# Gate weight blocks of a SwiGLU stage multiplied as seven half-size products instead of eight

## The reference

```python
def swiglu(x, w_gate, w_up, w_down):            # x: 512 x 1024, w_gate and w_up: 1024 x 2816, w_down: 2816 x 1024
    return (jax.nn.silu(x @ w_gate) * (x @ w_up)) @ w_down

x = x + 0.5 * swiglu(rms_norm_2(x, ffn1_norm[layer]), ...)
```

## Time and profile before

| | |
|---|---|
| median of 3 runs | 2524.61 us (2520.6 to 2525.54) |
| profiled execution, its own time | 2523.24 us |
| its span in the trace | 2521.4 us |
| granted TensorE clock | 0.996 of full speed |
| TensorE matmul busy | 2482.9 us, 98% |
| VectorE busy | 1000.6 us, 40% |
| ScalarE busy | 865.6 us, 34% |
| GpSimd busy | 1069.8 us, 42% |

### The profile page before, as it was taken

The page is one execution under the profiler, slowest core; times in us unless marked ns, Lnnn a source line. Parts: engine busy times, 40 slices in busy tenths (PEclk is TensorE's granted clock), DMA queues, the critical chain, the costliest instruction groups (busy, mean ns, idle before and its releaser), DMA issues.

```text
span 2521.4 us, 31320 instructions
## 1 busy us (share of the span) xinstructions
PE 2482.9 (98%) x12983; PEld 2048.2 (81%) x12983; DVE 1000.6 (40%) x1664; ACT 865.6 (34%) x1286; POOL 1069.8 (42%) x830
## 2 busy tenths in 40 slices
PE   8999999999999999999999999999999999999999
PEld 7889778876688888887788888888888888888887
DVE  5676445145572222456532222421313544322222
ACT  4433443246552222336632222422212322322221
POOL 4233345312254444433244444544444544444443
PEclk9999999999999999999999999999999999999999
DMA  4122103210143233312132332233332333233322
GB/s 143 60 68 94 34 26 118 84 51 20 49 129 100 88 98 99 94 57 72 44 105 96 99 101 92 92 101 101 100 100 72 112 100 100 84 100 101 100 89 79
DMA packets 215863, 217.66 MB, mean 86 GB/s; under 512 B 10615, under 2 KB 213106, under 8 KB 215722
## 3 DMA queue, kind: packets, MB, share of 16 engines
q1 hardware_dynamic: 215520, 215.61, 27.0%
q10 hardware_dynamic: 202, 0.06, 0.0%
HBM read 213.53 MB, written 2.12 MB: 86 GB/s over the span
## 4 chain that ended last, share of the span: by engine, by line
PE 94%; DVE 3%; ACT 2%; issue 1%; DMA 0%; SPq 0%; DVEq 0%; ACTq 0%
PE ps L516 73%; PE ps L509 6%; PE ps L519 5%; PE ps L513 2%; PE ps L869 2%; PE ps L904 1%; PE ps L886 1%; PE ps L2137 1%; PE ps L2198 1%; PE ps L1638 1%; ACT wh L475 0%; PE ps L538 0%; PE ps L1983 0%; PE ps L2003 0%; DVE NL L626 0%
## 5 line engine op out<-in xcount | busy, mean ns | idle before, releaser
L490 POOL TENSOR_TENSOR wl<-raw,wh 128x512 fp32r<-128x512 f32 x794 | 1040.0, 1342 | 1397.3 <-ACT wh L475 1382.9
L516 PE MATMUL ps<-NH,wh 128*128 128x512 f32 (+1 forms) x1824 | 716.3, 393 | 1.6 <-DVE NL L626 1.5
L516 PE MATMUL ps<-NL,wh 128*128 128x512 f32 (+1 forms) x1824 | 712.2, 390 | 0.0
L516 PE MATMUL ps<-NH,wl 128*128 128x512 f32 (+1 forms) x1824 | 711.9, 390 | 0.0
L475 ACT ACTIVATE wh<-raw 128x2048 fp32r<-128x2048 f32 (+3 forms) x218 | 378.9, 1738 | 475.1 <-PE ps L516 422.6
L516 PEld LDWEIGHTS ps<-NH,wh 128*128 128x128 f32 (+1 forms) x1824 | 343.0, 188 | 79.5 <-issue 6.4
L516 PEld LDWEIGHTS ps<-NL,wh 128*128 128x128 f32 (+1 forms) x1824 | 342.8, 188 | 73.7 <-issue 1.4
L516 PEld LDWEIGHTS ps<-NH,wl 128*128 128x128 f32 (+1 forms) x1824 | 342.7, 188 | 72.6
L516 PE MATMUL ps<-GH,wh 128*128 128x512 f32 x824 | 323.1, 392 | 0.0
L516 PE MATMUL ps<-GH,wl 128*128 128x512 f32 x824 | 320.7, 389 | 0.0
L516 PE MATMUL ps<-GL,wh 128*128 128x512 f32 x824 | 320.7, 389 | 0.0
(11 more groups left out here) (419 smaller groups left out, 2907.8 us busy)
## 6 DMA issues: line engine op xcount, KB each, us to landing
raw<-in_ffn_w_gate SPq DMA_DIRECT2D x44, 1024.0 KB, 5.3
raw<-in_ffn_w_up SPq DMA_DIRECT2D x44, 1024.0 KB, 5.3
raw<-in_ffn_w_down SPq DMA_DIRECT2D x32, 1024.0 KB, 5.1
raw<-in_w_in_ab SPq DMA_DIRECT2D x15, 1024.0 KB, 5.4
raw<-in_w_in_cd SPq DMA_DIRECT2D x14, 1024.0 KB, 5.0
raw<-in_ffn_w_down SPq DMA_DIRECT2D x16, 768.0 KB, 4.3
raw<-in_c_w_in SPq DMA_DIRECT2D x12, 1024.0 KB, 5.1
raw<-in_w_out_ab SPq DMA_DIRECT2D x8, 512.0 KB, 3.5
```

The source lines that it names most:

```text
L490: nc.gpsimd.tensor_tensor(wl[:, b % 2, ks, 0:w], raw[:, b % 2, ks, 0:w], wh[:, b % 2, ks, 0:w].bitcast(F32), ALU.subtract).then_inc(S("wei ...
L516: last = nc.tensor.matmul(ps[0:m1 - m0, bank, 0:SEQ], w[:, s, k, m0:m1], x(k), start=start, stop=stop)
```

## The change

From the third pair of a stage on (`SEVEN_FROM = 4` column tiles), the nine gate blocks of each of the four stages get the form "S". Such a block (1024 rows x 256 columns) is cut in four quarters A11 to A22 of 512 rows x 128 columns, the tokens' operand in four quarters B11 to B22 of 512 rows x 256 tokens. The two-by-two block product is formed from seven quarter products, with the sums S1 to S4 of the A quarters and T1 to T4 of the B quarters, instead of eight.

- The sums of weights are made for every S block: two by POOL, two by DVE. ACT then takes seven high parts, POOL seven low parts, of 128x512 elements each.
- The sums of tokens are made once a stage: eight tiles `bf` (H times the gain) by ACT, four differences by DVE, four high parts by ACT, four low parts by DVE, all in the time of the first two pairs, which keep the old form.
- TensorE adds the products into banks 0, 1 and 2. ACT copies the bank between products (`seven_copy`, three copies of 128x256 into `xs`), and DVE adds these later (`seven_dve`).
- ACT's list of a pair with an S block following: high parts of the next gate block now stand before the silus, and `seven_copy` of the next gate block stands behind the `GH` copies and ahead of the high part of the next up block.
- The F gates move to banks 0 and 1, the up units to 6 and 7, the down units of the first two groups to 4 to 7. The final gain of stage 0 moves from pairs 0 to 3 to pairs 2 and 3, four tiles in each.

The diff, without the buffers' places, the operand slices and the plain renamings of counts:

```diff
+LEFT = ("A11", "S1", "S2", "S4", "S3", "A12", "A22")
+RIGHT = ("B11", "T1", "T2", "B22", "T3", "B21", "T4")
+ACCUMULATOR = (0, 1, 0, 1, 0, 2, 0)
...
+            taken = (bank, bank + 1) if b.form == "W" else (0, 1, 2) if b.form == "S" else (bank,)
...
+    def seven_sums_pool(pool, b):
+        pool.wait_ge(S(f"raw_ready_{b % 2}"), RAWC[b])
+        nc.gpsimd.tensor_tensor(ssum[:, 2, :, :], seven_raw(b, "A11"), seven_raw(b, "A21"), ALU.subtract).then_inc(S("gate_sum"), 1)
+        nc.gpsimd.tensor_tensor(ssum[:, 0, :, :], seven_raw(b, "A21"), seven_raw(b, "A22"), ALU.add).then_inc(S("gate_sum"), 1)
+
+    def seven_sums_dve(dve, b):
+        n = SEVENS.index(b)
+        dve.wait_ge(S("gate_sum"), 2 * n + 1)
+        nc.vector.tensor_tensor(ssum[:, 1, :, :], seven_raw(b, "A22"), ssum[:, 2, :, :], ALU.subtract).then_inc(S("gate_mix"), 1)
+        dve.wait_ge(S("gate_mix"), 2 * n + 1)
+        nc.vector.tensor_tensor(ssum[:, 3, :, :], seven_raw(b, "A12"), ssum[:, 1, :, :], ALU.subtract).then_inc(S("gate_mix"), 1)
+
+    def seven_high(act, b):
+        n = SEVENS.index(b)
+        act.wait_ge(S(f"raw_ready_{b % 2}"), RAWC[b])
+        act.wait_ge(S("unit_done"), units_before(b - 1))
+        for name in LEFT:
+            if name == "S1":
+                act.wait_ge(S("gate_sum"), 2 * n + 2)
+            elif name == "S2":
+                act.wait_ge(S("gate_mix"), 2 * n + 1)
+            elif name == "S4":
+                act.wait_ge(S("gate_mix"), 2 * n + 2)
+            nc.scalar.activation(seven_left(b, name, wh, swh), seven_full(b, name), ACT.Copy).then_inc(S("weights_high"), 1)
+
+    def seven_pe(pe, b, f, first):
+        u, n = BLOCKS[b].unit0, SEVENS.index(b)
+        for j, (left, right) in enumerate(zip(LEFT, RIGHT)):
+            pe.wait_ge(S("weights_low"), LOW_BEFORE[b] + j + 1)
+            if left == "A11":
+                wait_slot(pe, u)
+            elif left in ("S2", "S4", "S3"):
+                pe.wait_ge(S("gate_copy"), 3 * n + ("S2", "S4", "S3").index(left) + 1)
+            elif left == "A22":
+                pe.wait_ge(S("gate_mid"), n + 1)
...
+            o = ps[:, ACCUMULATOR[j], 0:QN]
+            for k in range(QT):
+                for x, (w, e, plain, formed) in enumerate(((wh, swh, NH2, thi), (wh, swh, NL2, tlo), (wl, swl, NH2, thi))):
+                    last = nc.tensor.matmul(o, seven_left(b, left, w, e)[:, k, :], seven_right(right, plain, formed)[:, k, :],
...
+    def seven_copy(act, b):
+        n = SEVENS.index(b)
+        for x, bank in enumerate((0, 1, 0)):
+            act.wait_ge(S("gate_product"), 5 * n + x + 1)
+            nc.scalar.activation(xs[:, x, :], ps[:, bank, 0:QN], ACT.Copy).then_inc(S("gate_copy"), 1)
...
     def split_low(pool, b):
+        if BLOCKS[b].form == "S":
+            seven_sums_pool(pool, b)
+            seven_low(pool, b)
+            return
...
     def ffn_act(act, f):
         late_root_act(act, f"ffn{f}")
+        formed_base_act(act, f)
         for b0, t0, pairs in ffn_blocks(f):
+            if BLOCKS[b0].form == "S":
+                seven_copy(act, b0)
             for p_ in range(pairs):
                 u = BLOCKS[b0 + 2 * p_].unit0
+                if BLOCKS[b0 + 2 * p_].form == "S":
+                    split_high(act, b0 + 2 * p_ + 2)
                 for i in range(2):
                     act.wait_ge(S("evac_dve"), UNITS[u + i][1])
                     nc.scalar.activation(sg[:, i, :], sg[:, i, :], ACT.Silu).then_inc(S("gate_silu"), 1)
-                split_high(act, b0 + 2 * p_ + 2)
+                if BLOCKS[b0 + 2 * p_].form != "S":
+                    split_high(act, b0 + 2 * p_ + 2)
                 for i in range(2):
                     act.wait_ge(S("hidden"), FT * f + t0 + 2 * p_ + i + 1)
                     nc.scalar.activation(GH[:, 2 * p_ + i, :], tmp[:, i, 0:SEQ], ACT.Copy).then_inc(S("hidden_high"), 1)
+                if p_ + 1 < pairs and BLOCKS[b0 + 2 * p_ + 2].form == "S":
+                    seven_copy(act, b0 + 2 * p_ + 2)
                 split_high(act, b0 + 2 * p_ + 3)
+                if t0 + p_ == 0:
+                    formed_high_act(act, f)
...
     def ffn_dve(dve, f):
...
+                following = b0 + 2 * p_ + 2 if p_ + 1 < pairs and BLOCKS[b0 + 2 * p_ + 2].form == "S" else None
+                if BLOCKS[b0 + 2 * p_].form == "S":
+                    seven_dve(dve, b0 + 2 * p_, r)
+                    if following:
+                        seven_sums_dve(dve, following)
+                else:
...
                     if p_ == 0:
+                        formed_sums_dve(dve, f, ("T1", "T3", "T2", "T4"))
+                    else:
+                        formed_low_dve(dve, f)
+                    if following:
+                        seven_sums_dve(dve, following)
+                if f == 0 and t0 == 0 and p_ >= 2:
+                    if p_ == 2:
                         dve.wait_ge(S("norm_root"), roots_before["ffn0"] + 2)
                         step(dve, nc.vector.reciprocal(rstd[:, 0:SEQ], rstd[:, 0:SEQ]))
+                    for m in range(4 * (p_ - 2), 4 * (p_ - 2) + 4):
+                        final_gain_dve(dve, m)
...
+                if m == 5 and t0 != GROUPS[-1][0]:
+                    seven_sums_dve(dve, b0 + 2 * pairs + D // BC)
```

More of the change, by code:

```diff
@@ L182, in ffn @@
                 c = (t0 + 2 * q) * P
[L183 to L184 removed]
+                if t0 + 2 * q >= SEVEN_FROM:
+                    blocks.append(Block((f"ffn{which}_w_gate_2", layer), (0, D), [(c, BC, 0)], "DD", "S", [0, 0]))
+                else:
+                    blocks.append(Block((f"ffn{which}_w_gate_2", layer), (0, D), [(c, BC, 0)], "DD", "F", [0, 1]))
+                blocks.append(Block((f"ffn{which}_w_up_2", layer), (0, D), [(c, BC, 0)], "DD", "F", [6, 7]))
             for q in range(D // BC):
[L186 removed]
+                blocks.append(Block((f"ffn{which}_w_down_2", layer), (t0 * P, nt * P), [(q * BC, BC, 0)], "DD", "F",
+                                    [4 + 2 * (q % 2), 5 + 2 * (q % 2)] if t0 != GROUPS[-1][0] else None))
     ffn(0, 1, 0)
@@ L214, in weight_plan @@
             bank = b.bank[i] if b.bank else (unit + 2) % 4
-            taken = (bank, bank + 1) if b.form == "W" else (bank,)
-            slots.append((e, a if e == "A" else d, bank, sorted({held[x] for x in taken if x in held})))
+            taken = (bank, bank + 1) if b.form == "W" else (0, 1, 2) if b.form == "S" else (bank,)
+            slots.append((e, a if e == "A" else d, bank, sorted({held[x] for x in taken if x in held}) if b.form != "S" or i == 0 else []))
             for x in taken:
@@ L236, in bank_of @@
     return UNITS[u][2]
-LOW_BEFORE = [0]
-for _blk in BLOCKS:
-    LOW_BEFORE.append(LOW_BEFORE[-1] + -(-_blk.kts // 2))
+LOW_BEFORE, HIGH_BEFORE, SEVENS = [0], [0], []
+for _b, _blk in enumerate(BLOCKS):
+    LOW_BEFORE.append(LOW_BEFORE[-1] + (len(LEFT) if _blk.form == "S" else -(-_blk.kts // 2)))
+    HIGH_BEFORE.append(HIGH_BEFORE[-1] + (len(LEFT) if _blk.form == "S" else 1))
+    if _blk.form == "S":
+        SEVENS.append(_b)
 def low_count(b, k):
@@ L410, in program @@
     krr = at("krr", 39472, [P, NT, ROPE])
+    bf = at("bf", 34432, [P, KT, SEQ])
+    thi = at("thi", 34432, [P, 4, QT, QN], F32R)
+    tsum = at("tsum", 30336, [P, 4, QT, QN])
+    tlo = at("tlo", 30336, [P, 4, QT, QN], F32R)
+    swh = at("swh", 38528, [P, 3, QT, P], F32R)
+    swl = at("swl", 40064, [P, 3, QT, P], F32R)
+    ssum = at("ssum", 41600, [P, 4, QT, P])
+    xs = at("xs", 43648, [P, 3, QN])
     gcb = at("gcb", 29744, [P, 2, SEQ])
@@ L465, in blk_cols, with seven_raw, seven_full, seven_left @@
         return to + n
+    def seven_raw(b, name):
+        row, col = int(name[1]) - 1, int(name[2]) - 1
+        return raw[:, b % 2, QT * col:QT * col + QT, P * row:P * row + P]
+    def seven_full(b, name):
+        return seven_raw(b, name) if name[0] == "A" else ssum[:, int(name[1]) - 1, :, :]
+    def seven_left(b, name, tile, extra):
+        if name[0] == "A":
+            row, col = int(name[1]) - 1, int(name[2]) - 1
+            return tile[:, b % 2, QT * col:QT * col + QT, P * row:P * row + P]
+        return tile[:, b % 2, 0:QT, P:2 * P] if name == "S1" else extra[:, int(name[1]) - 2, :, :]
@@ new lines, in seven_right @@
+    def seven_right(name, plain, formed):
+        if name[0] == "B":
+            row, col = int(name[1]) - 1, int(name[2]) - 1
+            return plain[:, QT * row:QT * row + QT, QN * col:QN * col + QN]
+        return formed[:, T_ORDER.index(name), :, :]
+    def seven_sums_pool(pool, b):
+        pool.wait_ge(S(f"raw_ready_{b % 2}"), RAWC[b])
+        nc.gpsimd.tensor_tensor(ssum[:, 2, :, :], seven_raw(b, "A11"), seven_raw(b, "A21"), ALU.subtract).then_inc(S("gate_sum"), 1)
+        nc.gpsimd.tensor_tensor(ssum[:, 0, :, :], seven_raw(b, "A21"), seven_raw(b, "A22"), ALU.add).then_inc(S("gate_sum"), 1)
@@ new lines, in seven_low @@
+    def seven_low(pool, b):
+        for j, name in enumerate(LEFT):
```

(64 more changed lines are left out.)

19 lines of the change are left out of this document (added).

## The result

| | before | after | e6: both repairs |
|---|---|---|---|
| median, first measurement | 2522.61 us (4 runs) | 2541.07 us (2536.92 to 2541.16, 4 runs) | |
| ratio to before | | 1.0068 (1.0055 to 1.0080) | |
| median, beside the last experiments | 2521.66 us (12 runs) | 2536.09 us (4 runs) | 2499.68 us (6 runs) |
| ratio to before | | 1.0054 (1.0039 to 1.0069) | 0.9914 (0.9895 to 0.9932) |
| span of the profiled execution | 2521.4 us | 2539.0 us | 2497.5 us |

The changed kernel is slower: by 18.5 us in the first measurement, by 14.4 us in the second. 2553 us was forecast, so the sign and the mechanism came out as told and the stalls were set too long. One of the ten runs of e4 took 2855.02 us at a granted clock of 0.81; the ratios leave it out. The page of the changed kernel, to be laid beside the earlier trace rows: busy time of the engines, then the chain that ended last by engine.

What follows compares the result with a forecast made beforehand. TensorE, busy 98% of the span, was taken as the bound. On 2523.24 us, -28.8 + 35.4 + 12.0 + 8.8 + 1.2 + 0.8 = +29.4 gave 2552.6, stated as 2553; own range 2535 to 2570, chance 0.55.

Steps and rivals of the forecast that it cites:

- 36 S blocks: TensorE's gate blocks: 84 matmuls of 256 columns replace 48 of 512, saving 0.80 us each, -28.8 us if nothing waits.
- 15 ordinary links: Gate to next S gate within a group: third product stalls 2.36 us on ACT's first copy, +35.4 us.
- second pair, four stages: DVE's four low parts of T delay the first copy for the next S block, 3.0 us a stage, +12.0.
- gains in stage 0: Third pair of stage 0: reciprocal and four gains on DVE lengthen the loop to 29.8 us, +8.8.
- start of stage 0: Eight `bf` tiles and silus delay block 2's high part, so its first low part comes late, +1.2 us.
- first links of groups 2 and 3: First to second gate behind down blocks: 0.26 us of stall or none, taken as 0.1 us x 8, +0.8.
- The path of the loop: From third product through up block's preparation, DVE/POOL sums, high parts, silu, multiplies, `GH`, first copy, to next third product: 23.3 us.
- The list of signs: Trace signs expected: TensorE gap of some 2.4 us before the third product in each S block not first in its group.
- The rival that the waits for POOL do not bite: DVE's six two-input instructions take 0.69 us each, loop 20.7 us, no ordinary stall: 2498 us; chance 0.20.

Runs made afterwards that it cites:

- e6: Changed kernel with the first `seven_copy` copy ahead of the second `GH` and stage 0's gains moved to the down blocks; 2499.68 us, ratio to before 0.9914.
- e4: Changed kernel with only the last gate block of each stage as an S block; 2522.77 us, ratio to before 1.0005.
- e5: Changed kernel with POOL's last five low parts cut to 4 of 128 columns from each stage's second S block, products not right; 2513.27 us, ratio to before 0.9963.
- e1: Changed kernel with the first copy of the next gate block put between the two `GH` copies on ACT; 2506.16 us, ratio to before 0.9938.

## Why the prediction was right, step by step

| step | forecast | measured | from |
|---|---|---|---|
| 36 S blocks | -28.8 | -28.1 | 10.07 + 10.91 us a pair for 21.76 |
| 15 ordinary links | +35.4 (2.36 each) | +22.4 (1.49 each) | 22.47 - 20.98 |
| second pair, four stages | +12.0 | +7.3 | four waits named "issue", 6.4, and 0.2 each of the tail before |
| gains in stage 0 | +8.8 | +7.3, and 2.1 by the clock | third product to third product 28.30 - 20.98; 60 matmuls in 9.51 instead of 7.42 |
| start of stage 0 | +1.2 | +2.1 | third block of stage 0 |
| first links of groups 2 and 3 | +0.8 | 0 | 36 matmuls in 4.33 us |
| sum | +29.4 | +13.1 | stages: +13.4; 0.3 not assigned |

The path of the loop was right in each of its steps, and so was the place of the stall. (The list of signs asked for a gap in every S block that is not first in its group; the sum itself gave those second in groups 2 and 3 almost nothing, and they had none.) What was mis-sized is the term of the ordinary links: 23.3 us for the loop, 22.47 measured. Counted from the third product seen done, the silu ended at 14.9 us and not 15.25, and the second multiply at 19.7 and not 20.6; the waits for POOL in `GL` and the second multiply were 0.3 and 0.4 us, where I had 0.5 and 0.6. A loop 2.3 us longer than TensorE's own work and one 1.5 longer differ by 4% of the loop and by 37% of the stall: whoever subtracts two near numbers inherits the error of the larger. That is why both measurements, 2541 and 2536 us, lie 12 to 17 us under the 2553 of the forecast, in the lower part of its own range (2535 to 2570). The change's own 13.4 us on top of 2522.6 make 2536, 1 us inside that range, and 2.1 of them are a clock term that the forecast did not have: the sign and the path were earned, the place within the range is partly luck.

The second pair was set too long because DVE's list ahead of the copy was shorter: its four low parts took 6.81 us in stage 1, against 7.65 in my list, and the two multiplies ended 3.4 us apart instead of 3.8.

I listed no clock. The 2.1 us behind the long wait are the change's; what the clock did ahead of stage 0 is not.

The rival that the waits for POOL do not bite gave 2498, which the chip refuted for this order of lists. e5 has the 0.69 us durations of that rival in three of five places and comes to 2513, 8 us under the kernel before.

## What to carry to other kernels

When a change trades time of the bound engine for work on idle ones, add up not their shares but the longest closed path through their lists from one turn to the next, and compare that with the bound engine's turn; while the path is the longer one, it sets the time, and a further microsecond saved on the bound engine is worth nothing there. An instruction that the bound engine waits for belongs ahead of everything in its queue that depends on a long chain: here moving a 0.39 us copy ahead of one other instruction was worth some 30 us. Where the loop runs through engines that hold each other up, price each meeting by the remaining time of the other's instruction.

## What the runs showed that I had not expected

- A wait of TensorE of 7.1 us is followed by a lower granted clock (0.76 and 0.77 of full speed over 10 us, in two profiles; 1.00 where the wait was gone), worth 2.1 us. Shorter waits in the same place did it too: behind the 4.1 us of e1 and the 2.8 us of e5 the same 60 matmuls took 8.92 and 8.87 us instead of 7.43, at 0.84. The waits of 1.3 us, and the one of 2.35 us behind the second pair of stage 0, had no such effect: stages 1 and 2 repeat within 0.05 us between the two profiles.
- The clock also dips in the first 170 us in some executions and not in others of the same program; stage 0 started 6 us apart in two of them. Two kernels are better compared by the lengths of their stages than by their spans.
